# The last projection taken by halves of its input tiles, with two of its output pairs as seven block products

## What is computed

```python
y = jnp.concatenate([y_pool, y_m], axis=-1)        # (S, 2048)
h = h + jnp.einsum('bse,ed->bsd', y, w_out[l])     # the last projection
return rms_norm_2(h, norm_out_g)                   # mean over the 1024 channels of a token
```

## Time and profile before

| what | value |
|---|---|
| median of three runs | 1715.72 us |
| the profiled execution, its time / its span | 1714.43 / 1712.6 us |
| TensorE busy | 1670.5 us, 98% of the span, 8143 matmuls |
| VectorE / ScalarE / GpSimd busy | 1232.3 / 711.3 / 520.9 us |
| chain that ended last | TensorE 81%, VectorE 11%, ScalarE 3% |
| granted clock of TensorE, mean | 0.996 of full speed |

### The profile page before, as it was taken

One profiled execution on the slowest core, in us unless ns is written; L12 is line 12 of the kernel. 1 busy time (PEld: TensorE's weight loads), 2 busy tenths in 40 slices (PEclk: granted clock), 3 DMA queues, 4 the chain that ended last, 5 costly groups with the idle time before them and its releaser, 6 DMA issues.

```text
span 1712.6 us, 21708 instructions
## 1 busy us (share of the span) xinstructions
PE 1670.5 (98%) x8143; PEld 1380.4 (81%) x8143; DVE 1232.3 (72%) x1514; ACT 711.3 (42%) x918; POOL 520.9 (30%) x397
## 2 busy tenths in 40 slices
PE   8999999999999999999999999999999999999997
PEld 6888888887788888887888877788788788778885
DVE  8987888435677777777775799878888377897223
ACT  7211113235656655566622423511123767681003
POOL 5344544332201011010022332335344322214331
PEclk9999999999999999999999999999999999999999
DMA  6012125141010111101432354112227511346102
GB/s 230 25 74 74 49 96 202 59 173 37 25 38 1 38 38 37 38 1 37 171 107 99 121 185 155 62 54 81 74 88 236 210 50 71 115 144 249 50 13 99
DMA packets 48632, 158.63 MB, mean 93 GB/s; under 512 B 6144, under 2 KB 6784, under 8 KB 48272
## 3 DMA queue, kind: packets, MB, share of 16 engines
q1 hardware_dynamic: 48240, 156.72, 25.7%
q10 hardware_dynamic: 288, 0.52, 0.1%
HBM read 117.24 MB, written 39.98 MB: 92 GB/s over the span
## 4 chain that ended last, share of the span: by engine, by line
PE 81%; DVE 11%; ACT 3%; issue 2%; DMA 1%; SPq 1%; POOL 0%; DVEq 0%; POOLq 0%; ACTq 0%
PE pair L1169 27%; PE pair L1356 9%; PE pair L1430 9%; PE pair L1685 9%; PE pair L1493 5%; PE aux L1466 4%; PE pair L1479 3%; PE aux L1645 1%; PE pair L1244 1%; PE aux L1169 1%; PE pair L1851 1%; PE pair L1180 1%; PE pair L1188 1%; DVE stat_b L2901 1%; PE aux L1606 1%
## 5 line engine op out<-in xcount | busy, mean ns | idle before, releaser
L1005 POOL CAST w_hi<-w_raw 128x1024 fp32r<-128x1024 f32 x70 | 83.0, 1186 | 794.2 <-issue 562.9
L1007 POOL TENSOR_TENSOR w_lo<-w_raw,w_hi 128x1024 fp32r<-128x1024 f32 x70 | 179.9, 2570 | 5.6
L1169 PE MATMUL pair<-op_hi,w_hi 128*128 128x512 f32 x446 | 138.8, 393 | 1.3 <-ACTq L182 1.2
L1169 PE MATMUL pair<-op_lo,w_hi 128*128 128x512 f32 x446 | 137.7, 390 | 0.0
L1169 PE MATMUL pair<-op_hi,w_lo 128*128 128x512 f32 x446 | 137.5, 390 | 0.0
L2164 ACT ACTIVATE pt_hi<-pair 128x1024 fp32r<-128x1024 f32 x60 | 61.6, 1027 | 128.2 <-issue 84.4
L2533 DVE TENSOR_TENSOR pt_lo<-pair,pt_hi 128x1024 fp32r<-128x1024 f32 x60 | 73.5, 1224 | 53.5 <-ACT pt_hi L2164 50.0
L1430 PE MATMUL pair<-opb_hi,w_hi 128*128 128x512 f32 x256 | 101.9, 398 | 1.1 <-DVEq L182 0.6
L1169 PEld LDWEIGHTS pair<-op_hi,w_hi 128*128 128x128 f32 x446 | 83.6, 188 | 22.1 <-issue 3.3
L1430 PE MATMUL pair<-opb_hi,w_lo 128*128 128x512 f32 x256 | 100.2, 391 | 0.0
L1430 PE MATMUL pair<-opb_lo,w_hi 128*128 128x512 f32 x256 | 99.8, 390 | 0.0
(11 more groups left out here) (534 smaller groups left out, 4323.4 us busy)
## 6 DMA issues: line engine op xcount, KB each, us to landing
w_raw<-weight_units SPq DMA_DIRECT2D x106, 512.0 KB, 4.2
xa<-x_t SPq DMA_DIRECT2D x15, 512.0 KB, 7.2
xf<-y_dram SPq DMA_DIRECT2D x12, 512.0 KB, 4.6
x_dram<-xa SPq DMA_DIRECT2D x8, 512.0 KB, 6.3
xc<-x_dram SPq DMA_DIRECT2D x8, 512.0 KB, 8.7
x_dram<-xc SPq DMA_DIRECT2D x8, 512.0 KB, 2.8
u_dram<-u_rows SPq DMA_DIRECT2D x8, 512.0 KB, 5.3
c_dram<-c_rows SPq DMA_DIRECT2D x8, 512.0 KB, 2.8
```

The lines of the kernel that those rows point to most:

```text
L1005: pool.tensor_copy(w_hi[:, half, :], w_raw[:, u % RAW, :]).then_inc(w_hi_done, 1)
L1007: pool.tensor_tensor(w_lo[:, half, :], w_raw[:, u % RAW, :], w_hi[:, half, :], ALU.subtract).then_inc(w_split, 1)
L1169: mm = pe.matmul(acc[:, cols], w, x[:, kx, cols], start=(first and k == 0 and n == 0), stop=(last and k == KT - 1 and n == 2))
```

## The change

All eight output rows are first multiplied with tiles 0 to 7 and copied to xf (units 92 to 99), then all with tiles 8 to 15 (units 100 to 107). Rows 4 to 7 of the first half are two pairs (units 96 and 97, 98 and 99) of seven products. Their input differences are loaded as blocks from y3_dram. The last two rows are computed by token halves: left of row 6, left of row 7, right of row 6, right of row 7. Tiles 8 to 15 go through DRAM, the last two as well, and into places that earlier tiles leave; the rows of x pass through one buffer, x_row. POOL_LAST becomes (3, 4, 5). The core of the diff:

```diff
-SECOND = [BASE[4] + offset for offset in PAIRED]
+PAIRED3 = (4, 6)
+SECOND = [BASE[4] + offset for offset in PAIRED] + [BASE[5] + offset for offset in PAIRED3]
-Y3_UNITS = [(e, i) for i in range(2) for e in range(3)] + [(e, i) for e in range(3, KT) for i in range(2)]
+Y3_UNITS = [(e, i) for i in range(2) for e in range(KT)]
```

SP's queue; `load_x_row(k)` waits for `residual(k - 1)`, since x_row is one buffer:

```diff
+            sp.wait_ge(skip_ready, 2 * MH)
+            for slot in range(4):
+                load_block3(slot)
             store_head(2)
+            for t in range(2):
+                store_y("y3", KT + 2 * LAST + t, out_last)
...
+            load_x_row(0)
+            weights_to(BASE[5] + 10)
+            sp.wait_ge(product_done, product_at(PAIR3 + 1, "P1"))
+            for k in range(KT, KT + 4):
+                load_low(k)
+            sp.wait_ge(product_done, product_at(PAIR3 + 1, "P6"))
+            for k in range(KT + 4, 2 * KT):
+                load_low(k)
+            weights_to(BASE[5] + 12)
+            for k in range(1, KT):
+                load_x_row(k)
+                weights_to(BASE[5] + 12 + k)
```

TensorE; `product2` waits for the blocks and weights as in the earlier projection:

```diff
+            for u in range(BASE[5] + 2, UNITS - 2):
+                if u in SECOND:
+                    for name in ORDER2:
+                        product2(SECOND.index(u), name)
+                elif not in_pair(u):
+                    i = Y3_UNITS[u - BASE[5]][1]
+                    unit(u, u, o_hi, o_lo, "y3", kt0=KT * i, slots=HI_SLOT, wait_operand=(u == BASE[5] + KT))
+            last_rows(UNITS - 2, o_hi, o_lo)
```

ScalarE; `partial_row` copies an accumulator to xf and frees it, `block3_hi` waits for the difference and for the stores of tiles 14 and 15:

```diff
+            partial_row(0)
+            partial_row(1)
+            block3_hi(0, "P5")
+            block3_hi(1, "P7")
+            partial_row(2)
+            block3_hi(2, "P6")
+            block3_hi(3, "P4")
+            partial_row(3)
+            partial_pair(PAIR3)
+            partial_pair(PAIR3 + 1)
             for k in range(KT, 2 * KT):
                 y3_hi(k)
...
             for half in range(2):
+                half_square(KT - 2, half)
+                half_square(KT - 1, half)
```

VectorE, behind the last `out_gate` (the low parts of tiles 8 and 9 stood ahead of it); `pair3_first_row` adds P3 and frees the accumulator, `residual(k)` scales x_row and adds it to xf[k], `half_sum` and `half_accumulate` are `add_residual` and `accumulate` for half the tokens:

```diff
+            for name in ("P5", "P7", "P6", "P4"):
+                block3_sum(name)
+            for n in range(3):
+                pair_sum(PAIR3, n)
+            block3_low("P5")
+            block3_low("P6")
+            pair_low(PAIR3, "P5")
+            block3_low("P7")
+            pair_low(PAIR3, "P6")
+            block3_low("P4")
+            pair_sum(PAIR3, 3)
...
+            pair_c11(PAIR3 + 1, partial_rows(PAIR3 + 1))
+            for k in range(8, 10):
+                y_low(k)
+            pair_c22(PAIR3 + 1, partial_rows(PAIR3 + 1))
+            for k in range(10, 12):
+                y_low(k)
+            pair3_first_row(PAIR3 + 1)
...
+            residual(0)
+            for k in range(KT - 2):
+                if k >= 1:
+                    accumulate(3, k - 1, sq_f, acc_f)
+                whole_sum(k)
+                residual(k + 1)
+            residual(KT - 1)
+            accumulate(3, KT - 3, sq_f, acc_f)
+            half_sum(KT - 2, 0)
+            half_accumulate(0)
+            half_sum(KT - 1, 0)
             dve.wait_ge(rstd_ready, 5)
+            for k in range(2):
+                final(0, k)
+            half_sum(KT - 2, 1)
+            for k in range(2, 4):
+                final(0, k)
+            half_accumulate(1)
+            for k in range(4, KT - 2):
+                final(0, k)
+            half_sum(KT - 1, 1)
```

More of the change, by code:

```diff
@@ L631, in space @@
         def space(job):
-            return aux[:, 0:S] if job == BASE[5] + 2 else pair[bank(job)][:, :]
+            return pair[bank(job)][:, :]
         def accumulator(q, name):
@@ new lines, in load_block3, with load_x_row @@
+            def load_block3(slot):
+                rows, half = T_PARTS[slot]
+                for n in (6, 7):
+                    sp.wait_ge(y_stored[n % 2], stored("y3", n))
+                sp.dma_start(t3_raw[:, slot, :, :],
+                             y3_dram[QUAD * rows:QUAD * (rows + 1), :, half * HALF:(half + 1) * HALF]
+                             .rearrange("k p c -> p k c")).then_inc(t_loaded[rows], 16)
+            def load_x_row(k):
+                if k >= 1:
+                    sp.wait_ge(shift_ready, MH + k)
+                sp.dma_start(x_row[:, :], x2_dram[k]).then_inc(x_loaded[k], 16)
@@ L969, in _ @@
             made = [0, 0]
-            for k in (0, 1, 4, 2, 5, 3, 7, 6):
+            for k in (0, 1, 3, 2, 4, 6, 5, 7):
                 made[k in POOL_LAST] += 1
@@ L1650, in mix, with operand2 @@
                     mm.then_inc(mix_done, 1)
+            def operand2(p, name, k):
+                if p < PAIR3:
+                    if name in T_SLOT:
+                        return t_hi[:, T_SLOT[name], k, :], t_lo[:, T_SLOT[name], k, :]
+                    return operands[name][0][:, k, :], operands[name][1][:, k, :]
+                if name in T_SLOT:
+                    return t3_hi[:, T_SLOT[name], k, :], t3_lo[:, T_SLOT[name], k, :]
+                tile = k if name == "P1" else QUAD + k
+                cols = slice(HALF, S) if name == "P3" else slice(0, HALF)
+                return o_hi[:, HI_SLOT[tile], cols], o_lo[:, LO_SLOT[tile], cols]
             def product2(p, name):
@@ L1895, in _ @@
             pe.wait_ge(state_ready, NDIR * (CH - 1) * MH)
[L1896 to L1910 removed]
+            first_pair(BASE[5], "y3", o_hi, o_lo, HI_SLOT, free=scan_read, between=turn_last, ahead=KT)
+            for u in range(BASE[5] + 2, UNITS - 2):
+                if u in SECOND:
+                    for name in ORDER2:
+                        product2(SECOND.index(u), name)
+                elif not in_pair(u):
+                    i = Y3_UNITS[u - BASE[5]][1]
+                    unit(u, u, o_hi, o_lo, "y3", kt0=KT * i, slots=HI_SLOT, wait_operand=(u == BASE[5] + KT))
+            last_rows(UNITS - 2, o_hi, o_lo)
         @block.scalar
@@ L2499, in _, with partial_row, block3_hi @@
                 norm_step(MH - 1, c)
+            def partial_row(e):
+                u = BASE[5] + e
+                act.wait_ge(unit_done, plain(u + 1))
+                act.wait_ge(op_ready, OP0["y3"] + e + 1)
+                link(act.activation(xf[:, e, :], pair[bank(u)][:, :], ACT.Copy), skip_ready)
+                signal(pair_free[bank(u)])
+            def block3_hi(n, name):
+                act.wait_ge(t_summed, T_SUMMED0 + T3 + n + 1)
+                for t in range(2):
+                    act.wait_ge(y_stored[t], stored("y3", 2 * KT - 2 + t))
+                link(act.activation(t3_hi[:, T_SLOT[name]], t3_raw[:, T_SLOT[name]], ACT.Copy), t_hi_made)
@@ L3483, in _ @@
                 out_gain(LAST, i, aux[:, i * S:(i + 1) * S])
-            for k in range(8, 10):
-                y_low(k)
             dve.wait_ge(ln_done, MH)
@@ L3488, in _, with block3_sum, block3_low @@
                 out_gate(LAST, i)
-            for k in range(10, 16):
+            def block3_sum(name):
+                slot = T_SLOT[name]
+                minuend, other = {"P5": (1, 0), "P7": (2, 1), "P6": (2, 0), "P4": (3, 2)}[name]
+                for rows in range(2):
+                    dve.wait_ge(t_loaded[rows], T3_LOADED)
+                link(dve.tensor_tensor(t3_raw[:, slot], t3_raw[:, minuend], t3_raw[:, other], ALU.subtract), t_summed)
+            def block3_low(name):
+                slot = T_SLOT[name]
+                dve.wait_ge(t_hi_made, T_HI0 + T3 + ("P5", "P7", "P6", "P4").index(name) + 1)
+                link(dve.tensor_tensor(t3_lo[:, slot], t3_raw[:, slot], t3_hi[:, slot], ALU.subtract), t_low)
@@ new lines, in _ @@
+            for name in ("P5", "P7", "P6", "P4"):
[9 more added lines that the diff above has]
+            pair_sum(PAIR3, 3)
+            pair_low(PAIR3, "P7")
+            pair_low(PAIR3, "P3")
+            pair_c11(PAIR3, partial_rows(PAIR3))
+            for n in range(2):
+                pair_sum(PAIR3 + 1, n)
@@ L3490, in _ @@
+            for k in range(10, 12):
+                y_low(k)
+            pair3_first_row(PAIR3 + 1)
+            y_low(12)
+            pair3_second_row(PAIR3 + 1)
+            for k in range(13, 16):
                 y_low(k)
```

186 lines of the change are left out of this document (103 added, 83 removed).

## The result

The changed kernel takes 1718.28 us (median of 18 runs, 1716.34 to 1720.52), the kernel before 1715.24 us in the same comparison (18 runs, 1712.95 to 1717.13): a ratio of 1.0018 with a 95% interval of 1.001 to 1.0025. It is 3.0 us slower, within the 0.2% (3.4 us) that the prediction took as the bound of "the same"; the interval lies wholly above 1, so the small loss itself is clear of noise.

The account below looks back on a forecast made before the run. TensorE, busy nearly all the span, was taken to bound the kernel. Terms -5.4 + 2.6 + 0.9 + 4.1 = +2.2 us on the median of three runs, 1715.72, gave 1717.9 us, range 1713.2 to 1721.8.

Parts of the forecast that it names:

- The removed matmuls: Last projection: two pairs of units need 168 matmuls instead of 2 x 96, 24 fewer at 0.2267 us, -5.4 us.
- Start of the first pair: VectorE's operands for the first pair's products come late: +2.3 us at P5, +0.3 behind it; bounds 0.4 to 4.0.
- the wait of 2 to 3 us ahead of P5: Sign in the changed profile: TensorE waits 2 to 3 us for VectorE before product P5; none would refute the contention.
- differences of 128x2048 beside GpSimd: Sign at the first pair: if these VectorE operations cost no more beside GpSimd than alone, the prediction is most wrong.
- The ninth unit: After the second pair, VectorE's low parts beside GpSimd's split delay the accumulator-freeing sum: +0.9 us, 0 to 1.5.
- The first statistics: Tail, first half: row 7 of x is loaded late, so the second statistics sum begins late, +2.7 us.
- The last half sum's window: Tail, second half: extra half sum and half accumulate, behind a square after three scalings, delay the last half sum, +1.4 us.
- Rival B: TensorE's clock falls in the new waits at the pair and tail: +5.0 us in all, 1720.7 us; chance 0.27.
- Rival A: Pair start and statistics turn out covered, waits under 2.0 us in all: 1710.3, or 1712 us; chance 0.12.
- Rival C: Blocks later than 1552 or tiles 8 to 15 later than 15 us add their lateness; chance 0.03.

Follow-up runs that it names:

- e11: e5 with VectorE's block sums P5 and P7 moved ahead of the last two gate products; 1710.04 us, ratio 0.997.
- e9: e8 with the tail orders of e1 and e2 added; 1714.91 us, ratio 0.9999.
- e3: Changed kernel with the sum that frees the ninth unit's accumulator moved ahead of the low part of tile 11; 1717.74 us, ratio 1.001.
- e2: Changed kernel, right half: row 6 squared before ScalarE's three scalings, final products 4 and 5 behind VectorE's last half sum; 1716.63 us, ratio 1.0011.
- e1: Changed kernel with the scaled rows of x worked off one row ahead; 1714.79 us, ratio 0.9999.
- e5: Changed kernel with the orders of e1, e2 and e3, and each weight low part right behind its product's block low part; 1711.15 us, ratio 0.9975.
- e4: Changed kernel with the weight low parts for P5 and P6 each right behind its block low part; 1717.26 us, ratio 1.0013.
- e8: Changed kernel with all sixteen units plain (no blocks, no seven products), tiles 8 to 15 loaded and split earlier; 1719.08 us, ratio 1.0025.
- e6: Changed kernel with two of the four block loads moved behind the store and mz's loads in SP's queue; 1723.95 us, ratio 1.0051.
- e10: Changed kernel with VectorE's block sums P5 and P7 moved ahead of the last two gate products; 1717.36 us, ratio 1.0014.

## Why the prediction was right, point by point

It gave 1717.9 us, range 1713.2 to 1721.8, "the same" as the likeliest; 1718.28 came. The sign of the sum and its parts held, with two sizes too small and one right for a wrong reason. That the two times are only 0.4 us apart is in part luck. The +2.2 was added to a median of three runs, 1715.72, and the median of all eighteen is 1715.24. Difference against difference, +2.2 was forecast and +3.0 came in the medians, +3.6 in the profiles.

- **The removed matmuls, -5.4.** Shown by the busy count (24 fewer) and by e11 against e9 (4.8 of it reaches the end, where one wait of 0.3 us is left).
- **Start of the first pair, +2.6 forecast, 2.4 measured; right in size, wrong in its working.** I kept the end of the gate products at 1552.1; it was 1550.35 (0.5 us of this is the earlier start of the whole stage), because the load of mz's rows let them start only after GpSimd's subtraction. I wrote that this load "finds the queue empty by then": its landing grew by 1.4 us. From there to the end of P5's weight low part it is 18.7 us, where I had 17.0 and 2.2 of contention. The contention of 1.1 us for a subtraction was nearly right (1.3), its place was not: slowed to 3.2 us itself, and behind casts of 2.75 and 2.59 us, the second subtraction came beside low P7 and P6's weight low part, which took 4.30 us instead of 3.06. So 0.9 came at P5 and 1.5 at P6, where I had put 2.3 and 0.3. I had slowed VectorE by GpSimd and left GpSimd at its old speed. The errors cancelled, and that is luck too: of the signs named, the wait of 2 to 3 us ahead of P5 did not come (0.61, and 1.29 ahead of P6), and differences of 128x2048 beside GpSimd cost 0.3 us more than alone, near the "no more" that would have refuted it.
- **The ninth unit, +0.9 forecast, 1.7 measured** (1.4 of wait and 0.3 in the slow start behind it). The contention was as charged (two low parts took 4.58 us instead of 2.46, 2.1 for my 2.0), but they began 0.5 us later than I had them, at 1602.30: the sum ahead of them stood behind two other low parts. Just over the bound of 1.5; e3 shows the cause.
- **The first statistics, +2.7 forecast, 3.9 measured: the term that was mis-sized.** The second sum began 2.8 us late, as worked out. What I left out is the price behind it. ScalarE's table load, once covered, now stands between the late square and the logarithm: 0.5 us, and the logarithm comes at T + 18.7 and T + 19.0 in e3 and e2, where the clock stayed up. And where the clock falls it is T + 19.4. e1 shows that the late row of x is the cause of all of it: its logarithm is at T + 15.6 again. (The prediction calls T the end of the eleventh whole unit; it is the fourteenth unit, and the time 1675.12 is the right one.)
- **The last half sum's window, +1.4 forecast, 1.4 measured**, of which 0.3 came back behind it. e2, e5, e9 and e11 show it: 21.4 to 21.8 us from the logarithm to the end instead of 23.1.
- **Rival B, the clock.** It happened in the statistics, but its working does not hold. I took the length of the wait for what decides, from one wait of 2.94 us behind which the clock fell. The same wait, in the same code, is in all twelve profiles (2.93 to 2.96 us), and in the changed kernel the first product behind it is quick:

```profile
1227.10 0.50 PE L1737 MATMUL pair<-t_hi,w_hi 128*128 128x512 f32 x1 [2.94 <-DVE w_lo L3120]
```

It is slow (0.79 or 0.80 us) in five profiles: before, e4, e5, e8 and e9. In e2 and e11 the clock fell 1 to 2 us later, and in the other five it stayed at full speed for the next 4 us. The statistics show the same: waits of 1.99 to 2.11 us brought the clock to 0.50 in the changed kernel, e4, e6, e8 and e10, but 1.93 and 2.25 did not in e3 and e2. The Trainium skill (TensorE: Matmul & The Clock Gate, part 1) has the clock follow how busy the engine has been recently. The rows do not isolate that: the code ahead of the wait of 2.94 us is the same each time, and the outcome differs. What decides stays open. Ahead of the pair the clock never fell but in e6. The price was small: 0.5 to 0.65 us in the statistics (ScalarE's idle time ahead of the logarithm, 0.47 to 0.65), 2.9 us in e6.
- **Rival A** needed waits under 2.0 us. The change as written could not have it, but e11 does, 5.3 us faster, from other orders of the same work.
- **Rival C** did not happen in the changed kernel and is what e6 made happen.

Left open by the runs: what sets how VectorE and GpSimd share the time when their work overlaps (VectorE's 1.23 us becomes 3.30 beside one GpSimd subtraction, its 2.29 beside another only 2.58). The Trainium skill (GPSIMD Engine Reference, Specifications) names contention for VectorE instructions with two SBUF inputs, which all of these are; the trace agrees that they contend, and shows what each loses; no run here varied that by itself. But the starts and ends shown above fit the two taking turns, operation by operation: the one that starts later gets nothing done until the other's is over. GpSimd's subtraction of 1557.88 starts inside a VectorE difference (1557.36, 2.58 us) that ends at 1559.94, and 1559.94 + 1.29 = 1561.23, where 1561.10 is measured. Of the two low parts of 1602.30 the first takes 1.23 us; the second starts at 1603.56, inside the subtraction that ends at 1605.79, and 1605.79 + 1.23 = 1607.02, where 1606.88 is measured. The residual row of 1674.77 starts inside the subtraction that ends at 1676.97, and 1676.97 + 1.29 = 1678.26, where 1678.06 is measured. So a loss would go by what is left of the other engine's operation, not by one's own length, and a long operation of VectorE loses little because it makes GpSimd wait. This is worked out after the fact, to within 0.2 us in these three places.

## What to carry to other kernels

Before a block of work is moved in a hand-written queue, look at what the old order had filled by chance: the two low parts that moved away had covered a load, and a single row buffer that was harmless between whole rows became a serial round trip of 10.6 us (residual, load, residual, 1674.77 to 1685.41) at the end. Price such chains buffer by buffer, and try cheap reorderings one by one and together before judging the algorithm: here the same 24 saved matmuls were worth 0.8 us in one order and 4.9 in another. When a gap is filled, ask what it had kept apart.

## What the runs showed of the hardware

- VectorE and GpSimd at work in the same stretch: both lose, and unequally. Half-unit subtractions on GpSimd took 3.2 us instead of 1.29 while VectorE's 128x2048 operations lost 0.3 each and its 128x512 ones 1.0; whole-unit ones cost a 128x1024 operation of VectorE 2.1 us and took 3.3 to 4.3 instead of 2.4 themselves.
- Behind waits of about 2 us in the statistics TensorE was granted 1.2 GHz in five profiles and kept 2.4 GHz in two, with waits of 1.93 and 2.25 us. Behind one and the same wait of 2.94 us in an unchanged stretch it was at 1.2 GHz at once in five of twelve profiles, 1 to 2 us later in two, and not within 4 us in five. After 5.25 us it made products at 1.2 GHz for some 5.6 us.
- ScalarE's load of the logarithm's table took 1.28 us, 1.6 with the step behind it. Done by 1689.16 it cost the kernel before nothing, and behind the late square it cost 0.5.
- 512 KB loads that landed in 4.8 to 5.6 us took 6.2 to 7.0 behind four of 1 MB.
